# Gain and bias of the last norm: two broadcast loads replaced by two row loads, four matmuls and four copies

## What is computed

```
def layer_norm(x, g, b):
    mu = mean(x);  var = mean((x - mu) ** 2)
    return (x - mu) * rsqrt(var + LN_EPS) * g + b

h = moe_ffn(x, w_router, b_router, w_gate_up, b_gate_up, w_down, b_down)
x = layer_norm(DEEPNORM_ALPHA * x + h, ln3_g, ln3_b)
```

## Time and profile before

| | us |
|---|---|
| median of 3 runs (1206.78 to 1207.22) | 1207.15 |
| the profiled execution | 1207.5 |
| its span (first to last instruction) | 1205.6 |
| TensorE busy in it | 1148.1 |
| VectorE busy | 221.0 |
| ScalarE busy | 132.7 |
| GpSimd busy | 49.7 |

### The profile page before, as it was taken

How to read it: one execution, slowest core, us unless ns; L and a number is a source line. 1 busy time by engine, 2 the same in 40 slices (tenths; PEclk the granted TensorE clock), 3 DMA queues, 4 the chain that set the end, 5 groups by cost and what they waited for, 6 DMA issues and landing times.

```text
span 1205.6 us, 12958 instructions
## 1 busy us (share of the span) xinstructions
PE 1148.1 (95%) x5354; PEld 521.5 (43%) x5354; DVE 221.0 (18%) x560; ACT 132.7 (11%) x280; POOL 49.7 (4%) x56
## 2 busy tenths in 40 slices
PE   9999999999999999999999999898989899999986
PEld 7686746754434343433333443333333333333322
DVE  1233112224211111121111111111111111111114
ACT  2133102221100000001000000000000000000001
POOL 0232003010000000000000000000000000000001
PEclk9999999999999999999999999999999999999998
DMA  9953333397999999999999999999999999999995
GB/s 351 315 209 140 138 120 132 134 354 301 430 426 428 427 427 425 429 430 427 427 430 427 427 427 429 428 429 428 428 428 429 428 428 429 429 428 428 429 427 210
DMA packets 55411, 446.63 MB, mean 370 GB/s; under 512 B 10273, under 2 KB 11441, under 8 KB 30161
## 3 DMA queue, kind: packets, MB, share of 16 engines
q1 hardware_dynamic: 52912, 439.96, 87.9%
q10 hardware_dynamic: 2464, 6.18, 1.4%
HBM read 445.06 MB, written 1.07 MB: 370 GB/s over the span
## 4 chain that ended last, share of the span: by engine, by line
PE 61%; DMA 35%; DVE 2%; issue 1%; ACT 0%; SPq 0%
DMA ring<-in_w_gate_up 32%; PE bank L1673 22%; PE bank L1317 9%; PE bank L1698 9%; PE bank L1304 8%; DMA ring<-in_w_down 3%; PE bank L1557 3%; PE bank L1618 2%; PE bank L1633 1%; PE bank L1338 1%; PE bank L1744 1%; PE bank L1687 1%; PE bank L1502 1%; PE bank L1480 1%; DMA ring<-in_w_in 1%
## 5 line engine op out<-in xcount | busy, mean ns | idle before, releaser
L1673 PE MATMUL bank<-ring,PT 128*64 128x512 f32 x1848 | 409.2, 594 | 30.2 <-DMA ring<-in_w_gate_up 30.2
L1673 PEld LDWEIGHTS bank<-ring,PT 128*64 128x64 f32 x1848 | 129.7, 137 | 303.6 <-issue 242.4
L1166 DVE TENSOR_SCALAR reg_k<-bank 128x512 f32<-128x512 f32 x32 | 22.1, 692 | 455.0 <-PE bank L1673 455.0
L1304 PE MATMUL bank<-reg_bc,ring 128*128 128x256 f32 x448 | 99.7, 381 | 1.8 <-ACT reg_bc L717 1.8
L786 ACT ACTIVATE reg_v<-reg_k 128x512 f32<-128x512 f32 x30 | 18.9, 630 | 690.7 <-DVE reg_k L1166 690.7
L1698 PE MATMUL bank<-reg_q,NCt 128*64 128x512 f32 x400 | 92.5, 605 | 0.0
L1304 PEld LDWEIGHTS bank<-reg_bc,ring 128*128 128x128 f32 x448 | 84.2, 190 | 15.8 <-issue 4.8
L1698 PE MATMUL bank<-reg_bc,NCt 128*64 128x512 f32 x400 | 90.1, 592 | 0.0
L1557 PEld LDWEIGHTS bank<-L,reg_a 128*128 128x128 f32 x512 | 62.9, 196 | 24.8 <-issue 23.5
L1557 PE MATMUL bank<-L,reg_a 128*128 128x128 f32 x512 | 69.3, 288 | 1.0 <-DVE L L1080 0.7
L1197 DVE COPY reg_v<-bank 128x512 f32<-128x512 f32 x28 | 19.4, 692 | 269.0 <-PE bank L1698 269.0
(11 more groups left out here) (230 smaller groups left out, 693.1 us busy)
## 6 DMA issues: line engine op xcount, KB each, us to landing
ring<-in_w_gate_up SPq DMA_DIRECT2D x115, 2048.0 KB, 23.6
reg_bc<-in_w_down SPq DMA_DIRECT2D x26, 2048.0 KB, 20.7
reg_q<-in_w_down SPq DMA_DIRECT2D x25, 2048.0 KB, 19.2
ring<-in_w_down SPq DMA_DIRECT2D x9, 2048.0 KB, 19.0
ring<-in_w_in SPq DMA_DIRECT2D x5, 2048.0 KB, 17.7
reg_kv<-in_w_gate_up SPq DMA_DIRECT2D x5, 2048.0 KB, 18.5
reg_q<-in_w_gate_up SPq DMA_DIRECT2D x4, 2048.0 KB, 14.8
ring<-in_w_down SPq DMA_DIRECT2D x7, 1024.0 KB, 7.8
```

What stands on the lines that cost most here:

```text
L1166: nc.vector.tensor_scalar(gbuf, banks[0][:, :], LIMIT, None, ALU.min).then_inc(g_ready, 1)
L1304: last = mm(B(name)[:, a * T:(a + 1) * T], w[:, k, c:c + P], src[:, k, :], start=(k == 0), stop=(k == KD - 1))
L1673: last = mm(ps[half * CAP:(half + 1) * CAP, :], xgT[:, k, i * CAP:(i + 1) * CAP], w[:, j, col:col + HALF], start=False, stop=(k == KD - 1) ...
```

## The change

ScalarE no longer loads gain and bias into all partitions. It loads each row once, into partition 0 of the same tiles. TensorE spreads a row in the last pair: a matmul of a row of ones (128 columns, `one[0:1, :]`) with half a row (512 columns) puts that half into all 128 partitions of a bank, one half in `gate_ps` and the other in `up_ps`; ScalarE copies the two banks over the tile. The gain goes first, behind the transposes of the last expert; the bias behind the first expert's down product, when ScalarE has copied the gain (`ln3_spread`). The norm's readers wait for `ln3_spread` to be 4.

```diff
-            pool.wait_ge(ln_in[2], 32)
+            pool.wait_ge(ln3_spread, 4)
...
-            load_ln(2, ln3_g, ln3_b)
+            act.dma_start(x_nat[0:1, 0, :], ln3_g).then_inc(ln_in[2], 16)
+            act.dma_start(x_nat[0:1, 1, :], ln3_b).then_inc(ln_in[2], 16)
...
             pair(NE // 2 - 1, last=True)
+            for r in range(2):
+                act.wait_ge(ln3_rows, r + 1)
+                for half, ps in enumerate((gate_ps, up_ps)):
+                    nc.scalar.activation(x_nat[:, r, half * HALF:(half + 1) * HALF], ps[:, :], ACT.Copy).then_inc(ln3_spread, 1)
...
-            dve.wait_ge(ln_in[2], 32)
+            dve.wait_ge(ln3_spread, 4)
...
+            def spread_ln3(r):
+                if r == 0:
+                    pe.wait_ge(ln_in[2], 32)
+                    pe.wait_ge(gu_read, NE)
+                else:
+                    pe.wait_ge(ln3_spread, 2)
+                for half, ps in enumerate((gate_ps, up_ps)):
+                    last = mm(ps[:, :], one[0:1, :], x_nat[0:1, r, half * HALF:(half + 1) * HALF], start=True, stop=True)
+                last.then_inc(ln3_rows, 1)
...
+                def second_result():
+                    transpose_h(p * 2 + 2)
+                    spread_ln3(0)
...
-                final_down(p, 0, xy_ps, hT, lambda: transpose_h(p * 2 + 2))
+                final_down(p, 0, xy_ps, hT, second_result)
+                spread_ln3(1)
...
                 gather(0)
+                pe.wait_ge(ln3_spread, 4)
                 biases(NE, 0)
```

More of the change, by code:

```diff
@@ L361, in hybrid_layer @@
         tile_done, further_done = sem("tile_done"), sem("further_done")
+        ln3_rows, ln3_spread = sem("ln3_rows"), sem("ln3_spread")
         nmr3_ready, xhat3_ready = sem("nmr3_ready"), sem("xhat3_ready")
```

## The result

| | before | changed |
|---|---|---|
| median, 6 runs each | 1207.18 us | 1211.9 us |
| lowest to highest | 1206.78 to 1208.47 us | 1210.03 to 1213.06 us |
| ratio (95% interval) | | 1.0037 (1.0026 to 1.0047) |

By the ratio the change costs 4.5 us (3.1 to 5.7 us). I had forecast 1208.35 us, with a range of 1206.0 to 1210.3 us: the sign of the sum was right, its size far too small, and the measured time lies outside the range.

What follows compares the result with a forecast made beforehand. The weight stream was taken to bound until 1180.88 us, then TensorE's tail. Lead -1.85, gain spread +1.27 and bias spread +1.76 made +1.2 us on 1207.15 us: 1208.35 us, range 1206.0 to 1210.3 us.

Steps and rivals of the forecast that it cites:

- The stream bounds until 1180.88 us: Expert weights in one never-empty queue set the pace until TensorE's last wait, 0.49 us; TensorE then runs without a gap.
- Part 1, the lead: Dropping the two broadcast loads at 287 us brings the weight stream forward, 1.85 us of it kept to the end.
- A queue with 2.46 us left is still safe: A transfer issued that long before its predecessor lands loses nearly nothing; so the 4.3 us queue at 450.59 us keeps 1.85 us.
- Part 2, the price of a spread: On TensorE in the last pair, 1.76 us a spread: gain costs 1.27 us after 0.49 us of wait, bias 1.76 us.
- Rows do not change a matmul: TensorE's one-row spread matmuls cost as much as full ones, 0.86 to 0.885 us each; columns decide.
- rival (a): Removed loads were hidden, lead lost where the queue runs dry (297 or 450 us), both spreads paid: +3.0 us, 1210.2 us; chance 0.13.
- Part 3, ScalarE and the waits for the copies: ScalarE's four copies, 2.4 us, its later table load and the norm's waits for the copies cost nothing.
- (b): Rival: the stream's whole lead of 2.7 us is kept, starts needing under 1.6 us: +0.3 us, 1207.5 us; chance 0.12.
- (c): Rival: one-row matmuls overlap on TensorE, two spreads take 2 x 1.06 us: -0.2 us, 1206.95 us; chance 0.10.
- (d): Rival: TensorE waits for transfers behind 1180 us, hiding both spreads; the 2.7 us lead shows in full: 1204.45 us; chance 0.05.

Runs made afterwards that it cites:

- rows only: Kernel before with the two broadcast loads replaced by two row loads, no spreads: 1207.34 us, ratio 0.9993 to the kernel before.
- spreads of 128 rows: Kernel before plus spreads and copies, broadcast loads kept, each spread matmul the identity times the whole tile: 1211.15 us, ratio 1.0025 to the kernel before.
- one row, four times: Kernel before plus copies and one-row spreads, each spread's two matmuls done four times, broadcast loads kept: 1235.24 us, ratio 1.0223 to the kernel before.
- 128 rows, four times: Kernel before plus copies and 128-row spreads, each spread's two matmuls done four times, broadcast loads kept: 1221.65 us, ratio 1.0111 to the kernel before.
- experiment 4: Changed kernel with both spreads moved into the pair before the last, behind transposes and ahead of the down product: 1207.98 us, ratio 0.9996 to the kernel before.
- experiment 2: Kernel before with the spreads and copies added, gain and bias still coming as broadcast loads: 1212.36 us, ratio 1.0031 to the kernel before.

## Why the stream gained nothing

The lead was to be 1.8 to 2.7 us at 300 us and to be cut to 1.85 us by the short queue at 450 us. It never came to that. The three half chunks issued at 288.82, 292.25 and 293.97 us landed 2.6, 1.9 and 1.4 us earlier than before. The chunk issued at 297.40 us then landed 0.5 us later than before. SP's issues in the changed kernel (timeline) and their time to landing:

```profile
293.97 0.33 SPq L475 DMA_DIRECT2D ring<-in_w_down  x1
297.40 0.33 SPq L469 DMA_DIRECT2D ring<-in_w_down  x1
```

```profile
ring<-in_w_down SPq DMA_DIRECT2D x1, 1024.0 KB, 6.4
...
ring<-in_w_down SPq DMA_DIRECT2D x1, 2048.0 KB, 9.7
```

When that chunk was issued, the one ahead of it still had 293.97 + 6.4 - 297.40 = 3.0 us to go. In every kernel of this study the same chunk is issued at the same point of TensorE's program. In the eight where nothing else new is issued beside it and the transfers at 287 us are those of the kernel before or of the changed one, this table comes from the same two rows of each:

| kernel | left in the queue at the issue, us | own landing behind its predecessor's, us |
|---|---|---|
| changed | 3.0 | 6.7 |
| rows only | 3.5 | 5.7 |
| spreads in pair 14 | 3.3 | 7.2 |
| before | 4.4 | 4.8 |
| spreads alone | 5.1 | 4.9 |
| spreads of 128 rows | 4.9 | 4.8 |
| one row, four times | 4.6 | 4.9 |
| 128 rows, four times | 5.4 | 4.8 |

A chunk alone is 4.9 us of bytes. The three kernels without the broadcast loads issue it into 3.0 to 3.5 us of queue and lose 0.8 to 2.3 us; the five with them have 4.4 us and more and lose nothing. For this chunk the pattern is the same in all eight traces. That the short queue is the reason is argued, not shown, and 4.4 us are not a safe depth elsewhere: the next chunk lands 5.6 to 6.3 us behind this one in three of the five kernels with the loads, with 6 to 7 us left in the queue, and in the changed kernel the chunk issued at 400.00 us lands 6.2 us behind its predecessor with 15 us left.

The bytes say where the megabyte went. From 286 to 307 us ScalarE's queue moved 0.14 MB instead of 1.18 MB, 1.04 MB less, and SP's queue 6.42 MB instead of 6.06 MB, only 0.36 MB more. The rest, 0.68 MB, became idle time of the DMA engines: their busy share was 0.69 in 289 to 290 us (1.06 before) and 0.83 to 0.93 in 292 to 295 us (0.96 to 1.07 before). So most of what the two loads moved there had cost the stream nothing. The 0.36 MB, 0.8 us at 428 GB/s, hardly show in the landings, which wait for the last of a chunk's parts. Probably some of the sixteen engines had fallen behind the others; the trace does not name them, so this is not shown.

Behind that the landings of the two kernels still move against each other by up to 1.2 us. The changed kernel's are 0.1 us earlier for the chunk issued at 309.65 us and 0.2 us for that at 346.10 us, then 0.5 us later (issued at 400.00 us), 1.0 us later (497.56 and 576.87 us), 0.2 us later (751.98 and 1077.90 us), and 0.5 us later for the last chunk of expert 30, which lands at 1181.35 us against 1180.9 us. In the rows-only kernel that chunk lands at 1180.3 us, with the spreads in pair 14 at 1182.5 us, and in the four kernels that keep the loads and have nothing else new in the stream between 1180.4 and 1181.8 us. So at the end no lead is left that stands out from the differences between executions. The work and the transfers of these kernels before 297 us are the same but for the two loads, and their last landings differ by some 2 us, which is of the size of the 3 us by which runs of the kernel before differ. That the one is the cause of the other is likely, and not shown: only one execution of each kernel has a trace.

## The prediction, step by step

- *The stream bounds until 1180.88 us, TensorE behind it.* Right. Spreads in the pair before are free (experiment 4), and of the two in the last pair all but the 0.49 us of wait is paid (experiment 2).
- *Part 1, the lead.* This step failed: the term of -1.85 us. The last chunk of expert 30 landed 0.5 us later than before and not 1.85 us earlier; with the row loads alone it landed 0.6 us earlier, and the time fell by 0.8 us (between 1.9 us less and 0.2 us more). A half chunk's 7.5 us against 5.0 us was right about that half chunk, which took 4.9 us in the changed kernel. The failure begins one transfer on. The bytes were counted as if all that ScalarE's queue moved behind 289 us had been taken from the stream; by 307 us SP's queue was only 0.36 MB ahead, where I had 0.78 MB. And I looked for the shortest queue "after 300 us" and found the 4.3 us at 450.59 us, but the queues at 292.23 and 297.38 us were as short (4.1 and 4.4 us), and the lead itself made them shorter, by its own length.
- *"A queue with 2.46 us left is still safe."* Wrong, and the reason the lead was thought to survive. It rested on one pair of rows, at 267.29 us; with 3.0 to 3.5 us left three kernels lost 0.8 to 2.3 us. The kernel before had 4.4 and 4.3 us at 297 and 450 us and lost nothing there, which I could have read as the bound that its trace supports, in place of going below it.
- *Part 2, the price of a spread.* Right in kind, low by nearly a tenth: 1.91 us and not 1.76 us, within my upper bound of 1.95 us. The cover of 0.49 us was there. Together 3.3 us, where I had 3.03 us.
- *Rows do not change a matmul.* Right for its own time, and wrong for what runs behind it: in the profiled executions the clock fell after the one-row matmuls and the next chunk took 1.8 us more. This is the second step that failed: the sum had the matmuls behind a spread at no extra cost, and no rival had the clock in it. The range ended at 1210.3 us, where rival (a) stood; with the clock's 1.8 us behind it that is 1212.1 us, the measured 1211.9 us.
- *Part 3, ScalarE and the waits for the copies.* Right that they cost nothing: 9 us of idle time are left ahead of the norm.
- *Rival (a), the loads were hidden and both spreads are paid.* That is what happened as far as it goes, at the first of the two places named there (297 us), but its 1210.2 us lack the clock. I gave it 0.13, since I took 4.3 us of queue for more than enough.
- *Rivals (b), (c) and (d).* Out: no lead was kept, two spreads took 3.8 us and not 2.1 us, and the kernel is slower.

## What to carry to other kernels

A transfer that nobody waits for is free or dear by its time: here the same 1.05 MB cost next to nothing while the stream restarted at 287 us, 2.1 us at 297 us, and brought 2.5 us when the free slot was given to weights that are needed 890 us later. Before reckoning with a lead, follow it through the very next issues and subtract it from each queue, starting with those beside the removed load. Put added matmuls where the engine still waits for something, not in the tail; and do not spread a row by matmuls of one row where the clock matters.

## What the runs showed of the hardware

- Matmuls of one row keep TensorE busy by the records, and its granted clock can fall all the same. Sixteen records of them took 10.84 us (clock 0.50 for most of it), with 128 rows 6.87 us (clock 1.00). Two spreads of one row in pair 14 brought no fall. The Trainium skill (TensorE: Matmul & The Clock Gate, What's actually happening) says that the clock is set by how busy TensorE has been recently. With busy time as the records show it, these two runs do not agree: it is 4.00 us of 4.00 us in both from 1184 to 1188 us, at 0.50 with one row and at 1.00 with 128.
- The time of a matmul hardly depends on its rows: 1.91 us for two of one row, 1.72 and 1.92 us for two of 128 rows, at full clock.
- The chunk issued at 297 us landed 5.7 to 7.2 us behind its predecessor with 3.0 to 3.5 us of transfers left in its queue (three traces), and 4.8 to 4.9 us behind with 4.4 us or more left (five). Chunks elsewhere landed 5.6 to 6.3 us behind with 6 to 15 us left.
